# Placement of the shared region in one decoder layer: its start 64 bytes behind a multiple of 512, and the low operands of the second feed-forward matmul further on

## What is computed

```python
mod = silu(c) @ w_ada + b_ada                      # shifts, scales and gates
h   = rms_norm(x, g_pre_mix) * (1 + sc1) + sh1
u_lru, u_gate, q, k, v, f = split(h @ w_in)        # combined input projection
y_lru = rg_lru(conv4(u_lru)) * gelu(u_gate)
y_att = causal_attention(q, k, v, forget bias from f)
x   = x + gt1 * rms_norm([norm(y_lru) | norm(y_att)] @ w_out, g_post_mix)
h   = rms_norm(x, g_pre_mlp) * (1 + sc2) + sh2
x   = x + gt2 * rms_norm(relu(h @ w_ff1)**2 @ w_ff2, g_post_mlp)
```

## Time and profile before

| | |
|---|---|
| median of 3 runs | 2127.21 us (2126.25 to 2127.85) |
| the profiled execution: its time | 2129.04 us |
| its span | 2127.3 us |
| PE busy | 2051.6 us, 96% |
| DVE busy | 1615.4 us, 76% |
| ACT busy | 797.5 us, 37% |
| granted TensorE clock, mean | 0.99 |
| read from memory | 313.20 MB, 152 GB/s over the span |

### The profile page before, as it was taken

The page is one execution under the profiler, slowest core; times in us unless marked ns, Lnnn a source line. Parts: engine busy times, 40 slices in busy tenths (PEclk is TensorE's granted clock), DMA queues, the critical chain, the costliest instruction groups (busy, mean ns, idle before and its releaser), DMA issues.

```text
span 2127.3 us, 25152 instructions
## 1 busy us (share of the span) xinstructions
PE 2051.6 (96%) x9025; PEld 1671.2 (79%) x9025; DVE 1615.4 (76%) x1863; ACT 797.5 (37%) x1035; POOL 98.9 (5%) x105
## 2 busy tenths in 40 slices
PE   4999999999999999999999999999999999999997
PEld 4777778788778778888888888888888888888886
DVE  7998597875987887686776776876867867767766
ACT  5324612224553264343343343333333433433433
POOL 1001050000220001000000000000000000000000
PEclk8999999999999999999999999999999999999999
DMA  9975458856437763332333332333223323333333
GB/s 363 380 257 178 139 180 303 289 174 202 139 117 267 262 235 93 116 99 89 108 99 96 119 101 89 108 99 108 98 87 121 99 89 108 99 95 118 103 120 157
DMA packets 181582, 324.57 MB, mean 153 GB/s; under 512 B 12648, under 2 KB 49624, under 8 KB 179216
## 3 DMA queue, kind: packets, MB, share of 16 engines
q1 hardware_dynamic: 173600, 302.08, 43.5%
q0 software_dynamic: 3568, 16.95, 2.2%
q10 hardware_dynamic: 4352, 4.73, 0.7%
HBM read 313.20 MB, written 10.52 MB: 152 GB/s over the span
## 4 chain that ended last, share of the span: by engine, by line
PE 79%; DVE 13%; issue 3%; ACT 3%; DMA 2%; DVEq 0%; SPq 0%; ACTq 0%
PE pair L837 10%; PE pair L835 10%; PE pair L836 10%; PE pair L860 9%; PE pair L862 9%; PE pair L861 9%; PE bank L527 4%; PE bank L528 4%; PE bank L529 4%; PE bank L537 2%; PE bank L539 2%; PE bank L538 2%; DVE acc L1443 2%; DVE w_lo L1415 2%; DVE acc L1473 2%
## 5 line engine op out<-in xcount | busy, mean ns | idle before, releaser
L1863 DVE TENSOR_TENSOR yg<-yg,pair 128x1024 f32<-128x1024 f32 x240 | 289.6, 1217 | 287.5 <-PE pair L862 287.4
L835 PE MATMUL pair<-h_hi,w_lo 128*128 128x512 f32 x1020 | 397.5, 390 | 0.0
L837 PE MATMUL pair<-h_hi,w_hi 128*128 128x512 f32 x1020 | 396.8, 389 | 0.0
L836 PE MATMUL pair<-h_lo,w_hi 128*128 128x512 f32 x1020 | 396.8, 389 | 0.0
L860 PE MATMUL pair<-w_hi,op_lo 128*128 128x512 f32 x840 | 330.1, 393 | 8.9 <-DVE op_lo L1830 8.4
L861 PE MATMUL pair<-w_lo,op_hi 128*128 128x512 f32 x840 | 327.1, 389 | 0.0
L862 PE MATMUL pair<-w_hi,op_hi 128*128 128x512 f32 x840 | 327.1, 389 | 0.0
L965 ACT ACTIVATE w_hi<-raw 128x1024 fp32r<-128x1024 f32 (+1 forms) x114 | 118.4, 1044 | 295.6 <-DMA raw<-in_w_in_dram 175.5
L836 PEld LDWEIGHTS pair<-h_lo,w_hi 128*128 128x128 f32 x1020 | 191.4, 188 | 40.0 <-issue 0.2
L835 PEld LDWEIGHTS pair<-h_hi,w_lo 128*128 128x128 f32 x1020 | 191.5, 188 | 40.0 <-issue 0.2
L837 PEld LDWEIGHTS pair<-h_hi,w_hi 128*128 128x128 f32 x1020 | 191.5, 188 | 39.8
(11 more groups left out here) (272 smaller groups left out, 2769.7 us busy)
## 6 DMA issues: line engine op xcount, KB each, us to landing
raw<-in_w_ada_dram SPq DMA_DIRECT2D x128, 512.0 KB, 4.6
w_raw<-in_w_ff_dram SPq DMA_DIRECT2D x128, 512.0 KB, 3.8
raw<-in_w_ff_dram SPq DMA_DIRECT2D x128, 512.0 KB, 4.5
raw<-in_w_in_dram SPq DMA_DIRECT2D x74, 512.0 KB, 4.6
gst<-in_w_ada_dram SPq DMA_DIRECT2D x64, 512.0 KB, 7.1
raw<-in_w_out_dram SPq DMA_DIRECT2D x32, 512.0 KB, 4.7
x_tok<-in_x_dram SPq DMA_DIRECT2D x4, 1024.0 KB, 8.3
xr<-in_x_dram POOLq DMA_DIRECT2D x4, 1024.0 KB, 7.9
```

Source lines behind the costliest of these rows:

```text
L835: pe.matmul(b, lo[:, cols], h_hi[:, kt, :], start=(kt == 0), stop=False)
L836: pe.matmul(b, hi[:, cols], h_lo[:, kt, :], start=False, stop=False)
L837: last = pe.matmul(b, hi[:, cols], h_hi[:, kt, :], start=False, stop=(kt == KT - 1))
L1863: dve.tensor_tensor(y, y, pairs[2 + (i + r) % 2][:, :, :], ALU.subtract if i == 6 else ALU.add).then_inc(product_read, 1)
```

## The change

`to_line` grows from 56 to 72 floats, so the shared region starts 64 bytes later, at 80,448. `pad6`, which stands before `op_lo` and `u_raw` in their overlay, grows by 4 floats. The program itself holds the same instructions in the same order on every engine; the addresses alone differ.

```diff
-        sb("to_line", [P, 56])
+        sb("to_line", [P, 72])
...
         _, op_hi, s_tmp, _, op_lo, u_raw = overlay(
             ("pad5", [P, 64 * 256], F32), ("op_hi", [P, 7, 2, 256], F32R), ("s_tmp", [P, 2, 256], F32),
-            ("pad6", [P, 32 * 256], F32), ("op_lo", [P, 7, 2, 256], F32R), ("u_raw", [P, FT, COLS], F32))
+            ("pad6", [P, 32 * 256 + 4], F32), ("op_lo", [P, 7, 2, 256], F32R), ("u_raw", [P, FT, COLS], F32))
```

## The result

| | before | after |
|---|---|---|
| median of the runs | 2127.53 us (2126.25 to 2128.76, 4 runs) | 2155.81 us (2154.43 to 2157.99, 4 runs) |
| ratio to before, 95% interval | | 1.0134 (1.0116 to 1.0151) |
| profiled execution: time, span | 2129.04, 2127.3 us | 2156.86, 2155.1 us |

The time lies outside the range of 2092 to 2143 us, on the side to which I had given 0.25. The page of the kernel after shows where to look: DVE and ACT are busy for as long as before, PE for 32.5 us longer.

A forecast was written before the change was run, and what follows sets the result against it. PE, busy 96% of the span, was taken to bound the kernel. All terms were 0, so 2129.04 us profiled stayed 2129.0 us, less 1.8 us for the median: 2127.2 us, range 2092 to 2143 us.

The forecast's parts named there:

- What bounds the kernel: Whole kernel: PE, busy 96% of the span; 1 ns on each of 8,520 fp32r matmuls is 8.5 us, not covered.
- DVE, ACT: 0: DVE and ACT instructions: operand addresses change no durations, at most 1 us of DVE inside its free time; taken as 0.
- PE, float32: 0: Float32 matmuls and transposes on PE: neither operand's address is seen (590 against 591 and 592 ns); 0.
- PE, fp32r: 0: The 8,520 fp32r matmuls: no change from 226.7 ns each, taken from float32 rows, between bounds of -113 and +113 us.
- The stationary side by itself: Stationary loads on PE: 188 ns beside the matmul before, 39 ns to spare, so a moved start makes no wait.
- A rule against the first rival: fp32r matmuls: the skill page's separate read port for loads means no address can bring its 215.7 ns, 94 us less.
- Rival A: fp32r matmuls: moving stream and stationary load stop colliding once one side shifts; faster, 28 us, to 2099 us; chance 0.30.
- Rival B: L527 to L529, L835 to L837: moving operand touches five 512-byte pieces, not four; 15 us slower, 2142 us; chance 0.20.
- Rival C: Loads into gst, first 160 us: runs off the multiple cost 1/16 more; 6 us slower, 2133 us; chance 0.05.
- D: op_lo lies 32 bytes further than the region, not 16; a phase inside 32 bytes would be unmet, worth 0; inside the forecast.
- no change: Whole kernel: the forecast itself, no change to be seen, its own range 2123 to 2131 us; chance 0.45.

The follow-up runs named there:

- the other sign: Against the kernel before, stat grew and to_line shrank by 64 bytes: raw, w_hi, w_lo 64 bytes behind a multiple of 512, region on one; 2158.15 us, 1.0136.
- The sweeps: Two kernels without the layer, issuing rows of 32 or 30 fp32r matmuls with varied operand offsets, the second also fewer columns; 226.7 ns between starts at best.
- the region alone: Against the kernel before, only to_line grew, 56 to 72 floats: whole shared region, op_lo and u_raw included, 64 bytes later; 2158.84 us, 1.0140.
- distance 256: Against the kernel before, eps allocated ahead of raw, to_line left out: w_hi and w_lo 32 bytes behind a multiple of 512, region 288; 2133.67 us, 1.0023.

## Why the prediction was wrong

**What bounds the kernel** was right in the main: PE. But that nothing covers a change of what a matmul costs, so that each ns is worth 8.5 us, was too much. The distances of the changed kernel add up to 31.2 us (below) and the time grew by 28 us; those of the other sign add up to 40.8 us, and the time grew by 29.3 us.

**DVE, ACT: 0** was right: DVE's subtractions take 1219 and 1221 ns after the change, and ACT is busy for 797.0 us (797.5 before).

**PE, float32: 0** was right, 429.2 ns a record with both at +0, with moving +64 and with stationary +64.

**PE, fp32r: 0** is the step that failed. I had written that the trace cannot answer it, and then took the nearest row, the float32 ones, between ends of -113 and +113 us. Measured, from the table of groups:

```
L835-837   2862 x (230.25 - 226.73) = 10.1 us
L860-862   2325 x (231.88 - 227.16) = 11.0 us
L537-539   1125 x (233.33 - 227.63) =  6.4 us
L527-529   1563 x (229.07 - 227.24) =  2.9 us
L924-926    191 x (231.14 - 226.72) =  0.8 us
```

That is 31.2 us for PE alone (the counts include a few waits), while the span grew by 27.8 us. The difference is waits that shrank: PE's idle time, the span less its busy time, fell from 75.7 to 71.0 us. 3.0 us of it are the waits for op_lo at the start of a chunk: 8.4 us before, 5.4 us in the row of L860 after the change, since a slower PE gives DVE more time. In the stage from L835 to L924 the two sums of 10.1 and 11.0 us are 21.1 us and the stage grew by 17.6 us. The kernel with the other sign shows more of it: PE's idle time was 64.3 us, 11.4 us less than before, 5.0 of them at L860. That is about the gap between the 40.8 us of its distances and the 29.3 us that it lost. The estimates for it had counted matmuls alone.

**The stationary side by itself** (39 ns to spare, so 0) failed with it. The loads still take 188 ns and still end in time, and L537 to L539 and the products, whose stationary side moved, lost 5.7 and 4.7 ns a matmul. That a load fits into the time of the stream beside it does not mean that its place costs nothing.

**A rule against the first rival.** The Trainium skill (TensorE: Matmul & The Clock Gate, Step-by-step: what each phase is for) has the two reads on ports of their own, and says that the load takes no read bandwidth from the running matmul. The sweeps show that for fp32r at 512 columns the place of one against the other changes the time of a matmul, by up to 10 ns in 227; here the measurement decides. Where in the chip the two get in each other's way isn't shown.

**Rival A** had the right quantity, the difference of the two operands in the low address bits, and the wrong sign: I took the 13.3 ns for a collision of the two reads and the distance 0 for the bad case, and it is the best case. That the two reads collide at other distances is the natural reading, but no run shows a collision as such. Its argument against itself, that the two streams run at different rates and a fixed shift would clear at most a part, did not hold: a fixed shift of 64 bytes changed every row that had it, by 2.2 or 6.6 ns. **Rival B** came nearest in time, 2142 us, with a mechanism that is false: L860 to L862 would have kept 226.7 ns, and both sides at +64 would have cost as much as the moving side alone. **Rival C** was there: 1.5 to 4.4 us between the kernels with gst on and off a multiple of 512 whose matmuls are as before (143.8 and 144.5 against 146.0 to 148.2 us), where I had worked out 6 us. The first part of its working was right: the 1,024-byte packets took 8% longer (47.0 to 51.0 ns; I had 6%). The rule of the Trainium skill that I had named (DMA: Bandwidth & Descriptors, How a descriptor splits into AXI transactions) gives 6% as well, an estimate; it is worded for reads, while it is the write into SBUF that moved here. My evidence against this rival, that w1_raw lands no later than raw, had 2,048-byte packets in a stage with free queues. **D**, the 16 bytes that become 32, took place: it made the distance in the products smaller, 231.88 against 233.38 ns of the region alone. What 16 bytes would have done in the kernel was not run.

**The chances.** For a term of up to 8.5 us by the ns which no row showed, 0.45 on no change was too much. The nearest row was of another kind of matmul, and the tidy 226.7 ns of every one of 34 matmuls, all at one distance, could have been read as a hint that this placement was a special one.

## What to carry to other kernels

For fp32r matmuls of 512 moving and 128 stationary columns back to back, keep moving and stationary tensors a multiple of 256 bytes apart in their start addresses; where both lie against the lines of 512 does not matter to PE (226.7 ns at both +0 and, once settled, both +64). A pad or a small tensor put ahead of one of them can cost 1.4% of such a kernel without one instruction changed. One misplaced operand in three slows the matmuls behind it too. Loads feel their own place: 1,024-byte packets that start 64 bytes off took 8% longer. When a trace cannot show a term and 1 ns of it is worth more than the noise, a row of 30 matmuls for each placement tells it in one short run.

## What the runs showed of the hardware that I had not expected

- With fp32r, 512 columns: 226.7 ns between starts at a distance of 0 or 256 bytes (mod 256), 228.4 to 236.8 ns at all others that were tried, 228.4 at stationary +240, 228.9 at moving +12 and +64, 236.6 at +4. The single distances then follow a cycle (226, 229, 232 at moving +64; 231, 236 at stationary +64). Float32 matmuls of the same shape don't change (429.2 ns a record). Why 64 ahead is better than 64 behind, and why some pairs of the same distance differ by up to 3.5 ns, isn't explained by these runs.
- A cost of 13.1 to 13.3 ns for each fp32r matmul above 512, 384 or 256 columns at 2.4 GHz, alike for the three; with 128 columns a matmul takes 111.7 ns. What it is stays open.
- Fewer stationary columns (96, 64, 32) made a matmul at distance 0 slower, 230.0 to 231.8 ns.
- Packets of 1,024 bytes into SBUF took 47.0 ns at +0 and 51.0 ns at +64. Of the 3.7 us that the kernel with distance 256 lost ahead of L633 I can name only this; in the profile with gst alone moved that stage was 1.5 us longer, and the rest was not tried apart.
